# An 8-core encoder block on Trainium2: key latents multiplied from x times the norm's weight while x lands, with the root mean square applied afterwards

## The chip, the cores and the metric

The kernel runs on all 8 cores of one Trainium2 chip. Each core is given its own half of one sequence's queries (T = 1024 of S = 2048 tokens, batch 4) and works alone; no data goes between the cores. The metric is the time of one execution in microseconds (us) of the slowest core. The kernel before was run three times, 1668.05, 1668.99 and 1670.79 us; its median is 1668.99 us.

## The reference, cut to what matters

```
h = rmsnorm(x) * norm_g                       # over D = 2048 features
z = h @ w_in                                  # q_a (512), kv_a (256), k_pe (64), gates, conv inputs
q = rmsnorm(q_a, q_lat_g) @ w_uq              # 16 heads, own 1024 tokens
k, v = rmsnorm(kv_a, kv_lat_g) @ w_ukv        # 16 heads, all 2048 tokens
k_rope = k_pe, rotated by cos/sin(position)   # the "sine tables"
attn = softmax(q k) v ; conv branch ; gates ; two output projections
```

The change touches only the first two lines, for the columns kv_a and k_pe (the "key latents", 384 columns here with the rotated pair copied) and the sine tables. Since the norm is x * r(token) * norm_g(feature) with one r for each token, (x * norm_g) @ W * r is the same as h @ W, up to rounding.

## The kernel before, in words

All tensors lie transposed: features on the 128 partitions, tokens along the free dimension. x is read in four blocks of 512 tokens. Block 0 and 1 are the core's own tokens (queries and keys), 2 and 3 the other half (keys only). One block in float32 is 128 partitions x 16 feature chunks x 512 tokens (4 MB). There are two buffers, `xb[0]` for blocks 0 and 2 and `xb[1]` for blocks 1 and 3, so block 2 can be loaded once block 0 has been used up.

The program is a recording layer: each `P.op(engine, ...)` appends an instruction to its engine's queue in the order of the Python calls, and semaphore waits are derived from what is read and written. Every engine (PE, ACT, DVE, POOL, SP) executes its own queue strictly in that order. So the order of the work is the order in which the calls are written.

The first part, up to about 154 us, is what the change touches. Its helpers (line numbers are those of the kernel before):

- `load_x(blk, n)` (L327): the x block on SP's DMA queue in n pieces. `ld("pool", ...)` (L256) loads the weights `WlK` (key latents, 4 pieces) and `WlQ` (query latents, 4 pieces) from POOL's queue, which also turns float32 into bf16.
- `table(tab, posrow)` (L352 to L361): ten DVE instructions on 128x1024 float32 that depend on each other, then one sine on ACT (L362). `TABa` serves blocks 0 and 1 and the queries, `TABb` blocks 2 and 3.
- `A_sq(blk, j)`, j = 0 to 7: ACT squares two chunks of x (L383), and PE adds them up over the partitions with two matmuls by ones into bank `bB` (L385).
- `A_rs(blk)`: the factor r = exp(-0.5 ln(mean + eps)), two ACT instructions (L389, L390).
- `A_b(blk)`: sixteen DVE instructions `SCALAR_TENSOR_TENSOR` h = x * norm_g * r in bf16 (L401), into `hT` for blocks 0 and 1 (also used later by the gates and the convolution) and into `hTt` for blocks 2 and 3.
- `lat(blk, W, n, banks)`: 16 x n matmuls of 512 columns (L416), n = 3 for the key latents and 4 for the query latents, each waiting for its chunk of h.
- `e1_sq(blk)`: squares of the three key banks on ACT (L431, L445) and the product with the sine table on DVE (L446). `e1_mm` and `e2_mm` call `norm_of`: 2 or 4 matmuls by ones (L435), Ln and Exp on ACT (L436, L437), and 2 or 4 DVE instructions that write the normed latents (L439). `e1_ss` is four tiny matmuls (L454) and a copy (L456); `e1_cmb` a float32 matmul (L460) and an ACT copy (L461).
- `halo(blk)` (L407): one column of h of a neighbouring block, for the convolution.

The order before is, per block: all eight `A_sq`, `A_rs`, `A_b`, and only then `lat`. Both tables come first of all on DVE. The calls are L477 and the lines behind it: block 0's key latents, block 1's squares and norm, block 1's key latents, the two query latents (with block 2's squares in between), then the key latents of blocks 2 and 3. Behind them POOL's queue waits for x block 3 and loads the first weights of the next part (`load_kv`, `load_q`, `load_dense`), whose buffers `ring` overlay the position rows and `kf`, the scratch of `table`.

The next part (attention with convolution and gates mixed in, from L612 and L694 on) begins with the keys of head 0 directly behind the last `lat`; it and all that follows are not changed.

## Time and profile before

| | |
|---|---|
| median of three runs | 1668.99 us |
| the profiled execution's own time | 1669.85 us |
| its span on the slowest core (core 1) | 1668.3 us |
| spans of all 8 cores | 1662.0 to 1668.3 us |
| PE / DVE / ACT / POOL busy | 94% / 46% / 44% / 6% of the span |
| granted PE clock, mean | 0.987 of full on core 1 |
| data moved by DMA | 119.01 MB |

The span runs from the first to the last instruction of the profiled core; the execution's own time is 1.6 us longer, which lies around it. PE is the engine with the most work, and over the whole span it is nearly always busy. The first fortieths of the span (41.7 us each) are the exception: there the page shows PE busy 3, 6 and 9 tenths.

A row of the timeline reads: start, length, engine, line, operation, output<-input, shape, how many are merged, and in brackets the idle time of the engine before it and what ended that. Rows of groups give the number, the total, the mean of one, and the idle time ahead. Matmuls of 512 columns overlap, so two in a row last 0.59 us and each further one adds less than its own 0.38 us.

### The profile page before, as it was taken

To read this page: it belongs to the slowest core of one execution; us is meant where nothing else is said; L and a number is where in the kernel's file an instruction comes from. 1 tells how busy PE (TensorE), PEld (TensorE's weight loads), DVE (VectorE), ACT (ScalarE), POOL (GpSimd) and SP (SyncE) were. 2 spreads that over 40 slices of the span, in tenths; PEclk is the share of its full clock that TensorE was granted. 3 is DMA by queue.
4 is the path that set the end of the run, shared out by engine and by line. 5 is a ranking of instruction groups with operands and counts; after the bars stand their busy time and mean duration, and the time that the engine had idled before them with its cause. 6 is when DMAs were issued, how large, how long until landed. Compare 5 with 4: busy or idle time off the path is not lost.

```text
span 1668.3 us, 22689 instructions; the slowest of 8 cores (1662.0 to 1668.3 us)
## 1 busy us (share of the span) xinstructions
PE 1568.8 (94%) x7660; PEld 732.3 (44%) x7660; DVE 774.1 (46%) x999; ACT 737.8 (44%) x1234; POOL 94.1 (6%) x181
## 2 busy tenths in 40 slices
PE   3698999999999998999999999999999999999998
PEld 0144444444444444445445444444444444444443
DVE  6326377676666666776776211111111111243554
ACT  3344368777677777787776211011110101243211
POOL 0000000000000000000000110000100010000000
PEclk9799999999999999999999999999999999999999
DMA  9750321022101111211111673334433534974511
GB/s 253 207 123 13 58 39 33 7 36 35 33 14 32 33 27 20 39 28 18 20 26 26 120 143 60 70 65 87 84 69 69 89 70 85 222 165 80 119 69 70
DMA packets 37888, 119.01 MB, mean 71 GB/s; under 512 B 3984, under 2 KB 4112, under 8 KB 36240
## 3 DMA queue, kind: packets, MB, share of 16 engines
q0 software_dynamic: 25488, 82.85, 29.0%
q1 hardware_dynamic: 12288, 34.72, 6.4%
q8 instruction: 65, 1.06, 0.3%
q14 instruction: 47, 0.39, 0.1%
HBM read 192.00 MB, written 8.39 MB: 120 GB/s over the span
## 4 chain that ended last, share of the span: by engine, by line
PE 84%; ACT 5%; DVE 4%; issue 3%; DMA 2%; SPq 0%; ACTq 0%; DVEq 0%; POOL 0%; POOLq 0%
PE ps_o L833 5%; PE ps_s L773 5%; PE ps_s L775 5%; PE ps_s L968 4%; PE ps_s L930 3%; PE ps_o L891 3%; PE ps_s L900 3%; PE ps_s L872 3%; PE ps_s L894 3%; PE ps_s L891 3%; PE ps_a L900 3%; PE ps_o L894 3%; PE ps_s L416 2%; PE ps_a L694 2%; PE ps_b L897 2%
## 5 line engine op out<-in xcount | busy, mean ns | idle before, releaser
L780 ACT ACTIVATE arena<-ps_s,arena 128x512 bf16<-128x512 f32 x512 | 323.6, 685 | 50.7 <-PE ps_s L775 45.4
L820 DVE TENSOR_TENSOR arena<-arena 128x1024 f32<-128x1024 f32 x224 | 273.2, 1220 | 22.9 <-ACT arena L780 16.6
L773 PE MATMUL ps_s<-arena 128*128 128x512 bf16 x512 | 194.5, 380 | 9.8 <-ACT arena L780 9.5
L775 PE MATMUL ps_s<-arena 128*128 128x512 bf16 x512 | 194.5, 380 | 0.0
L833 PE MATMUL ps_o<-arena 128*128 128x512 bf16 x512 | 152.7, 380 | 1.2 <-ACT arena L836 1.2
L773 PEld LDWEIGHTS ps_s<-arena 128*128 128x128 bf16 x512 | 50.1, 98 | 78.2 <-issue 21.1
L775 PEld LDWEIGHTS ps_s<-arena 128*128 128x128 bf16 x512 | 50.1, 98 | 57.9 <-issue 0.7
L833 PEld LDWEIGHTS ps_o<-arena 128*128 128x128 bf16 x512 | 49.5, 98 | 39.4 <-issue 2.2
L903 ACT ACTIVATE arena<-ps_o 128x512 f32<-128x512 f32 x16 | 9.6, 597 | 129.3 <-PE ps_o L891 129.3
L905 DVE SCALAR_TENSOR_TENSOR arena<-arena,ps_s 128x512 f32<-128x512 f32 x16 | 11.0, 688 | 115.7 <-PE ps_s L897 115.7
L903 ACT ACTIVATE arena<-ps_s 128x512 f32<-128x512 f32 x16 | 9.6, 597 | 124.4 <-PE ps_s L891 124.4
L905 DVE SCALAR_TENSOR_TENSOR arena<-arena,ps_b 128x512 f32<-128x512 f32 x16 | 11.0, 688 | 115.4 <-PE ps_b L897 115.4
L953 ACT ACTIVATE arena<-arena 128x512 f32<-128x512 f32 x32 | 20.1, 629 | 97.4 <-DVE arena L952 97.4
L968 PE MATMUL ps_s<-arena 128*128 128x512 bf16 x272 | 62.8, 384 | 0.0
L875 DVE TENSOR_TENSOR arena<-arena 128x512 bf16<-128x512 bf16 x32 | 13.6, 426 | 95.6 <-ACT arena L874 95.6
L891 PE MATMUL ps_o<-arena 128*128 128x512 bf16 x256 | 57.9, 379 | 0.0
L891 PE MATMUL ps_s<-arena 128*128 128x512 bf16 x256 | 57.9, 379 | 0.0
L894 PE MATMUL ps_s<-arena 128*128 128x512 bf16 x256 | 57.9, 379 | 0.0
L900 PE MATMUL ps_s<-arena 128*128 128x512 bf16 x256 | 57.9, 379 | 0.0
L900 PE MATMUL ps_a<-arena 128*128 128x512 bf16 x256 | 57.9, 379 | 0.0
L894 PE MATMUL ps_o<-arena 128*128 128x512 bf16 x256 | 57.9, 379 | 0.0
L934 ACT ACTIVATE arena<-arena 128x512 bf16<-128x512 f32 x32 | 23.1, 721 | 77.5 <-DVE arena L933 77.5
(274 smaller groups left out, 2546.1 us busy)
## 6 DMA issues: line engine op xcount, KB each, us to landing
arena<-w_dense POOLq DMA_DIRECT2D x48, 512.0 KB, 5.4
arena<-w_merge POOLq DMA_DIRECT2D x48, 512.0 KB, 5.8
arena<-x_fm SPq DMA_DIRECT2D x20, 1024.0 KB, 24.7
arena<-w_pg POOLq DMA_DIRECT2D x16, 576.0 KB, 5.9
arena<-w_out POOLq DMA_DIRECT2D x16, 512.0 KB, 7.4
out<-arena SPq DMA_DIRECT2D x32, 256.0 KB, 2.0
arena<-x_fm SPq DMA_DIRECT2D x8, 512.0 KB, 13.3
arena<-w_q POOLq DMA_DIRECT2D x16, 256.0 KB, 3.5
```

The costliest lines, as they stand in the source:

```text
L416: "pe", lambda h: h.matmul(bks[m].ap, lhsT=W.ap[:, kc, m * 128:(m + 1) * 128], rhs=src, start=(kc == 0), stop=(kc == 15)),
L773: P.op("pe", lambda h, bk=bk, qs=qs: h.matmul(bk.ap, lhsT=Kb.ap[:, kt * 128:(kt + 1) * 128], rhs=Qa.ap[:, qs], start=True, stop=False), re ...
L775: P.op("pe", lambda h, bk=bk, qs=qs: h.matmul(bk.ap, lhsT=KrT.ap[:, kt * 128:(kt + 1) * 128], rhs=Qb.ap[:, qs], start=False, stop=True), r ...
L780: P.op("act", lambda h, sb=sb, qb=qb: h.activation(out=pt.ap[:, qb * 512:(qb + 1) * 512], in_=sb.ap, func=AF.Exp, scale=so.ap[:, kt:kt + 1 ...
L820: P.op("dve", lambda h, pt=pt, ac=ac: h.tensor_tensor(out=ac.ap, in0=ac.ap, in1=pt.ap, op=ALU.add), reads=R(ac, *pt.rl), writes=R(ac))
L833: P.op("pe", lambda h, qb=qb, kt=kt, pt=pt, hh=hh: h.matmul(Ow.ap[:, qb * 512:(qb + 1) * 512], lhsT=V.ap[:, kt, (hh % 2) * 128:(hh % 2) * ...
L872: P.op("pe", lambda h, kc=kc, bk=bk, sl=sl, ts_=ts_: h.matmul(bk.ap, lhsT=sl.ap[:, kc, :], rhs=hT.ap[:, kc, ts_], start=(kc == 0), stop=(k ...
L891: P.op("pe", lambda h, kc=kc, b_ma=b_ma, s_ma=s_ma, ts_=ts_: h.matmul(b_ma.ap, lhsT=s_ma.ap[:, kc, :], rhs=hT.ap[:, kc, ts_], start=(kc == ...
L894: P.op("pe", lambda h, kc=kc, b_mc=b_mc, s_mc=s_mc, ts_=ts_: h.matmul(b_mc.ap, lhsT=s_mc.ap[:, kc, :], rhs=hT.ap[:, kc, ts_], start=(kc == ...
L900: P.op("pe", lambda h, kc=kc, b_ya=b_ya, s_ba=s_ba, ts_=ts_: h.matmul(b_ya.ap, lhsT=s_ba.ap[:, kc, :], rhs=AT.ap[:, kc, ts_], start=(kc == ...
L930: P.op("pe", lambda h, kc=kc, bk=bk, sl=sl, ts_=ts_: h.matmul(bk.ap, lhsT=sl.ap[:, kc, :], rhs=merged.ap[:, kc, ts_], start=(kc == 0), sto ...
L968: P.op("pe", lambda h, kc=kc, bg=bg, sl=sl, ts_=ts_: h.matmul(bg.ap, lhsT=sl.ap[:, kc, :], rhs=h2T.ap[:, kc, ts_], start=(kc == 0), stop=( ...
```

## The change

1. **Order of loads.** POOL loads WlK at once (before: after the fifth piece of block 0). SP loads block 0's pieces 0 and 1, then the first position row, then pieces 2 to 7; block 1 comes in 8 pieces instead of 4; WlQ waits for the fifth of these eight; the second position row comes last.
2. **Key latents without the norm.** A new `A_x(blk, kc)` writes x * norm_g in bf16 (a `TENSOR_SCALAR` on DVE, L409 of the new file) into `hTt`, for all four blocks, and `lat(..., WlK, ...)` reads that. The matmuls no longer wait for r. In exchange `e1_sq` begins with three DVE instructions that multiply the three banks by r in place (L463). `A_b` (now L417, one chunk per call) remains for blocks 0 and 1 alone, and `halo` (L423, L424) works from x.
3. **Order of the work.** For every pair of chunks the calls are now: square, two `A_x`, then the six matmuls of these chunks, then the two sums of squares. Table A's ten instructions stand between the chunks of block 0. Block 0's latent norm and its sixteen `A_b` stand between the chunks of block 1, and behind them; block 1's `A_b` stand inside block 0's query latents. Table B moves behind `A_x` of block 2, its sine into block 3's squares. The loads of the next part's weights are written later, behind table B.

```diff
@@ -314,10 +314,10 @@
         Tpe = mk(196736, F32, [512], "Tpe")
         TABb = mk(198784, F32, [1024], "TABb")
         rq = mk(202880, F32, [512], "rq")
+        hgt = mk(204928, F32, [16, 1], "hgt")
 
         s_c = P.slot("consts")
         ld("sp", cols.ap, cols_d, cols, P.slot("cols"))
-        ld("sp", posrow[0].ap, pos_d[:, 0:1024], posrow[0], P.slot("pos0"))
 
         def load_x(blk, n=4, qs=None):
             b = xb[blk % 2]
@@ -331,17 +331,17 @@
             return last
 
         half = []
-        load_x(0, 8, range(3))
-        ld("sp", posrow[1].ap, pos_d[:, 1024:2048], posrow[1], P.slot("pos1"))
-        load_x(0, 8, range(3, 8))
-        half1 = half[0:1]
         for q in range(4):
-            ld("pool", WlK.ap[:, 4 * q:4 * q + 4, :], w_latk_d[:, 4 * q:4 * q + 4, :], WlK.rl[q], P.slot(f"wk{q}"), deps=half1)
+            ld("pool", WlK.ap[:, 4 * q:4 * q + 4, :], w_latk_d[:, 4 * q:4 * q + 4, :], WlK.rl[q], P.slot(f"wk{q}"))
+        load_x(0, 8, range(2))
+        ld("sp", posrow[0].ap, pos_d[:, 0:1024], posrow[0], P.slot("pos0"))
+        load_x(0, 8, range(2, 8))
         half[:] = []
         ld("sp", cmb.ap, cmb_d, cmb, s_c)
-        load_x(1)
+        load_x(1, 8)
         for q in range(4):
             ld("pool", WlQ.ap[:, 4 * q:4 * q + 4, :], w_latq_d[:, 4 * q:4 * q + 4, :], WlQ.rl[q], P.slot(f"wl{q}"), deps=half[0:1])
+        ld("sp", posrow[1].ap, pos_d[:, 1024:2048], posrow[1], P.slot("pos1"))
 
         P.op("dve", lambda h: h.memset(ones.ap, 1.0), writes=R(ones))
         P.op("dve", lambda h: h.memset(onesf.ap, 1.0), writes=R(onesf))
@@ -349,17 +349,19 @@
 
         def table(tab, pr):
             a, k = tab.ap, kf.ap
-            P.op("dve", lambda h: h.tensor_copy(out=a, in_=pr.ap), reads=R(pr), writes=R(tab))
...
-            P.op("dve", lambda h: h.tensor_scalar(out=a, in0=a, scalar1=PI_LO, scalar2=-PI_LO, op0=ALU.min, op1=ALU.max), reads=R(tab), writes=R(tab))
-            return lambda: P.op("act", lambda h: h.activation(out=a, in_=a, func=AF.Sin), reads=R(tab), writes=R(tab))
+            yield P.op("dve", lambda h: h.tensor_copy(out=a, in_=pr.ap), reads=R(pr), writes=R(tab))
...
+            yield P.op("dve", lambda h: h.tensor_scalar(out=a, in0=a, scalar1=PI_LO, scalar2=-PI_LO, op0=ALU.min, op1=ALU.max), reads=R(tab), writes=R(tab))
+
+        def sine(tab):
+            P.op("act", lambda h: h.activation(out=tab.ap, in_=tab.ap, func=AF.Sin), reads=R(tab), writes=R(tab))
 
         ring = [mk(82048 + 4096 * i, BF16, [16, 128], f"ring{i}") for i in range(4)]
         wq = [mk(208384, BF16, [4, 256], "wq0"), None]
@@ -381,36 +383,52 @@
         def A_sq(blk, j):
             b, sq = xb[blk % 2], sqx[j % 2]
             P.op("act", lambda h: h.activation(out=sq.ap, in_=b.ap[:, 2 * j:2 * j + 2, :], func=AF.Square), reads=R(b.rl[j]), writes=R(sq))
+
+        def A_ss(blk, j):
+            sq = sqx[j % 2]
             for i in range(2):
                 P.op("pe", lambda h, i=i: h.matmul(bB.ap, lhsT=ones.ap, rhs=sq.ap[:, i, :], start=(j == 0 and i == 0), stop=(j == 7 and i == 1)), reads=R(ones, sq), writes=R(bB))
+
+        def A_sqs(blk, j):
+            A_sq(blk, j)
+            A_ss(blk, j)
 
         def A_rs(blk):
             rs = rsb[blk % 2]
             P.op("act", lambda h: h.activation(out=rs.ap, in_=bB.ap, func=AF.Ln, bias=col(COL_EPS), scale=1.0 / D), reads=R(bB, cols), writes=R(rs))
             P.op("act", lambda h: h.activation(out=rs.ap, in_=rs.ap, func=AF.Exp, scale=-0.5), reads=R(rs), writes=R(rs))
 
+
+        def xsrc(blk, kc):
+            t = hTt[blk // 3]
+            return t.ap[:, kc, :], t.rl[kc]
+
+        def A_x(blk, kc):
+            b = xb[blk % 2]
+            dst, dres = xsrc(blk, kc)
+            P.op("dve", lambda h: h.tensor_scalar(out=dst, in0=b.ap[:, kc, :], scalar1=col(COL_NG + kc), scalar2=None, op0=ALU.mult), reads=R(b.rl[kc // 2], cols), writes=R(dres))
+
         def hsrc(blk, kc):
-            if blk < 2:
-                return hT.ap[:, kc, blk * 512:(blk + 1) * 512], hres(kc, blk)
-            return hTt[blk - 2].ap[:, kc, :], hTt[blk - 2].rl[kc]
-
-        def A_b(blk):
+            return hT.ap[:, kc, blk * 512:(blk + 1) * 512], hres(kc, blk)
+
+        def A_b(blk, c):
             b, rs = xb[blk % 2], rsb[blk % 2]
-            for c in range(16):
-                dst, dres = hsrc(blk, c)
-                P.op("dve", lambda h, c=c, dst=dst: h.scalar_tensor_tensor(out=dst, in0=b.ap[:, c, :], scalar=col(COL_NG + c), in1=rs.ap, op0=ALU.mult, op1=ALU.mult),
-                     reads=R(b.rl[c // 2], rs, cols), writes=R(dres))
+            dst, dres = hsrc(blk, c)
+            P.op("dve", lambda h: h.scalar_tensor_tensor(out=dst, in0=b.ap[:, c, :], scalar=col(COL_NG + c), in1=rs.ap, op0=ALU.mult, op1=ALU.mult),
+                 reads=R(b.rl[c // 2], rs, cols), writes=R(dres))
 
         def halo(blk):
-            t = hTt[blk - 2]
-            src, dst, m_ = (t.ap[:, :, 0:1], hT.ap[:, :, 1024:1025], COL_MR) if blk == 2 else (t.ap[:, :, 511:512], hT.ap[:, :, 1025:1026], COL_ML)
-            P.op("dve", lambda h: h.tensor_scalar(out=dst, in0=src, scalar1=col(m_), scalar2=None, op0=ALU.mult), reads=R(*t.rl, cols), writes=[hres(c, 2) for c in range(16)])
+            b, rs = xb[blk % 2], rsb[blk % 2]
+            t, c_, m_ = (0, 1024, COL_MR) if blk == 2 else (511, 1025, COL_ML)
+            P.op("dve", lambda h: h.tensor_tensor(out=hgt.ap, in0=b.ap[:, :, t:t + 1], in1=cols.ap[:, COL_NG:COL_NG + 16].rearrange("p (a b) -> p a b", b=1), op=ALU.mult), reads=R(*b.rl, cols), writes=R(hgt))
+            P.op("dve", lambda h: h.tensor_scalar(out=hT.ap[:, :, c_:c_ + 1], in0=hgt.ap, scalar1=rs.ap[:, t:t + 1], scalar2=col(m_), op0=ALU.mult, op1=ALU.mult),
+                 reads=R(hgt, rs, cols), writes=[hres(c, 2) for c in range(16)])
 
 
         def lat(blk, W, n, bks):
             out_ = []
             for kc in range(16):
-                src, sres = hsrc(blk, kc)
+                src, sres = xsrc(blk, kc) if W is WlK else hsrc(blk, kc)
                 for m in range(n):
                     out_.append(lambda kc=kc, m=m, src=src, sres=sres: P.op(
                         "pe", lambda h: h.matmul(bks[m].ap, lhsT=W.ap[:, kc, m * 128:(m + 1) * 128], rhs=src, start=(kc == 0), stop=(kc == 15)),
@@ -440,6 +458,9 @@
                      reads=R(bks[m], rq, cols), writes=R(dres))
 
         def e1_sq(blk):
+            rs = rsb[blk % 2]
+            for bk in (kbanks[blk][0], kbanks[blk][1], kbanks[blk][2]):
+                P.op("dve", lambda h, bk=bk: h.tensor_tensor(out=bk.ap, in0=bk.ap, in1=rs.ap, op=ALU.mult), reads=R(bk, rs), writes=R(bk))
             sq_of(kbanks[blk], 2)
             bp, tb_ = kbanks[blk][2], (TABa if blk < 2 else TABb)
             P.op("act", lambda h: h.activation(out=sqE.ap[:, 3, :], in_=bp.ap, func=AF.Square), reads=R(bp), writes=R(sqE.rl[3]))
@@ -472,29 +493,85 @@
         def e1_ins(blk):
             return [(9, lambda: e1_mm(blk)), (26, lambda: e1_ss(blk)), (32, lambda: e1_cmb(blk))]
 
-        table(TABa, posrow[0])()
-        sin_b = table(TABb, posrow[1])
+        def go(mms, lo, hi):
+            for f in mms[lo:hi]:
+                f()
+
+
+        tab = table(TABa, posrow[0])
         P.op("act", lambda h: h.activation(out=rq.ap[:, 0:1], in_=col(COL_EPS), func=AF.Ln), reads=R(cols), writes=R(rq))
+        mm = lat(0, WlK, 3, kbanks[0])
         for j in range(8):
             A_sq(0, j)
+            A_x(0, 2 * j)
+            A_x(0, 2 * j + 1)
+            if j > 1:
+                next(tab)
+            if j > 4:
+                next(tab)
+            go(mm, 6 * j, 6 * j + 6)
+            A_ss(0, j)
+        for _ in tab:
+            pass
         A_rs(0)
-        A_b(0)
+        sine(TABa)
+        e1_sq(0)
+
+
+        mm = lat(1, WlK, 3, kbanks[1])
+        for j in range(8):
+            A_sq(1, j)
+            A_x(1, 2 * j)
+            A_x(1, 2 * j + 1)
+            if j == 2:
+                e1_mm(0, banks[3])
+            elif j == 4:
+                e1_ss(0, banks[3])
+            elif j == 5:
+                e1_cmb(0)
+            if j != 2:
+                A_b(0, j if j < 2 else j - 1)
+            go(mm, 6 * j, 6 * j + 6)
+            A_ss(1, j)
+        A_rs(1)
+        for c in range(7, 11):
+            A_b(0, c)
+        e1_sq(1)
+        for c in range(11, 16):
+            A_b(0, c)
         load_x(2)
-        sin_b()
-        run(lat(0, WlK, 3, kbanks[0]), {})
-        e1_sq(0)
-        for j in range(3):
-            A_sq(1, j)
-        e1_mm(0, banks[3])
-        for j in range(3, 6):
-            A_sq(1, j)
-        e1_ss(0, banks[3])
-        e1_cmb(0)
-        for j in range(6, 8):
-            A_sq(1, j)
-        A_rs(1)
-        A_b(1)
+
+
+        mm = lat(0, WlQ, 4, qbanks[0])
+        go(mm, 0, 12)
+        e1_mm(1)
+        go(mm, 12, 20)
+        e1_ss(1)
+        go(mm, 20, 28)
+        e1_cmb(1)
+        for c in range(16):
+            A_b(1, c)
         load_x(3)
+        go(mm, 28, 64)
+        sq_of(qbanks[0], 4)
+        m4 = lat(1, WlQ, 4, qbanks[1])
+        mm = [m4[4 * kc + m] for kc in range(16) for m in range(3)] + m4[3::4]
+        go(mm, 0, 6)
+        e2_mm(0)
+        go(mm, 6, 16)
+        for j in range(8):
+            A_sqs(2, j)
+            A_x(2, 2 * j)
+            A_x(2, 2 * j + 1)
+            go(mm, 16 + 6 * j, 16 + 6 * j + 6)
+        A_rs(2)
+        sq_of(qbanks[1], 4)
+        tab = table(TABb, posrow[1])
+        for _ in tab:
+            pass
+        halo(2)
+        hTt.append(mk(32896, BF16, [16, 512], "hTt1"))
+        split(hTt[1], 16, "hTt1_")
         for i, b in enumerate(ring):
             b.slot = P.slot(f"ring{i}")
         wq[0].slot, wkv[0].slot = P.slot("wq0"), P.slot("wkv0")
@@ -504,22 +581,20 @@
         load_q(0)
         for s_ in range(4):
             load_dense(s_)
-        run(lat(1, WlK, 3, kbanks[1]), {})
-        e1_sq(1)
-        run(lat(0, WlQ, 4, qbanks[0]), ins(*e1_ins(1)))
-        sq_of(qbanks[0], 4)
-        m4 = lat(1, WlQ, 4, qbanks[1])
-        run([m4[4 * kc + m] for kc in range(16) for m in range(3)] + m4[3::4], ins((6, lambda: e2_mm(0)), *[(16 + 5 * j, lambda j=j: A_sq(2, j)) for j in range(8)]))
-        A_rs(2)
-        A_b(2)
-        sq_of(qbanks[1], 4)
-        halo(2)
-        hTt.append(mk(32896, BF16, [16, 512], "hTt1"))
-        split(hTt[1], 16, "hTt1_")
-        run(lat(2, WlK, 3, kbanks[2]), ins((5, lambda: e2_mm(1)), *[(14 + 4 * j, lambda j=j: A_sq(3, j)) for j in range(8)]))
+        mm = lat(2, WlK, 3, kbanks[2])
+        go(mm, 0, 5)
+        e2_mm(1)
+        go(mm, 5, 14)
+        for j in range(8):
+            A_sqs(3, j)
+            A_x(3, 2 * j)
+            A_x(3, 2 * j + 1)
+            if j == 1:
+                sine(TABb)
+            go(mm, 14 + 4 * j, 14 + 4 * j + 4)
+        go(mm, 46, 48)
         e1_sq(2)
         A_rs(3)
-        A_b(3)
         halo(3)
         run(lat(3, WlK, 3, kbanks[3]), ins(*e1_ins(2)))
         e1_sq(3)
```

At the start of PE's queue, before (L385 sums of squares, L416 key latents of block 0):

```order
L385 MATMUL ps_b<-arena 128x512 x16
L416 MATMUL ps_o<-arena 128x512 x2
L416 MATMUL ps_a<-arena 128x512
L416 MATMUL ps_o<-arena 128x512 x2
L416 MATMUL ps_a<-arena 128x512
```

The same place now (L434 is the latents' matmul, L390 the sum of squares):

```order
L434 MATMUL ps_o<-arena 128x512 x2
L434 MATMUL ps_a<-arena 128x512
L434 MATMUL ps_o<-arena 128x512 x2
L434 MATMUL ps_a<-arena 128x512
L390 MATMUL ps_b<-arena 128x512 x2
```

All sixteen sums stood ahead of the first latent matmul; now six latent matmuls and two sums alternate, eight times per block.

DVE's queue from the end of table A to block 1's norm, before (table B's ten stand directly ahead of the first row):

```order
L401 SCALAR_TENSOR_TENSOR arena<-arena 128x512 x16
L446 SCALAR_TENSOR_TENSOR arena<-ps_a,arena 128x512
L439 SCALAR_TENSOR_TENSOR arena<-ps_o,arena 128x512 x2
L456 COPY arena<-ps_s 128x4
L401 SCALAR_TENSOR_TENSOR arena<-arena 128x512 x16
```

And now, from the end of table A (L361) into block 1's chunks:

```order
L361 TENSOR_SCALAR arena<-arena 128x1024
L463 TENSOR_TENSOR ps_o<-ps_o,arena 128x512 x2
L463 TENSOR_TENSOR ps_a<-ps_a,arena 128x512
L467 SCALAR_TENSOR_TENSOR arena<-ps_a,arena 128x512
L409 TENSOR_SCALAR arena<-arena 128x512 x2
L417 SCALAR_TENSOR_TENSOR arena<-arena 128x512
L409 TENSOR_SCALAR arena<-arena 128x512 x2
L417 SCALAR_TENSOR_TENSOR arena<-arena 128x512
L409 TENSOR_SCALAR arena<-arena 128x512 x2
L457 SCALAR_TENSOR_TENSOR arena<-ps_o,arena 128x512 x2
L409 TENSOR_SCALAR arena<-arena 128x512 x2
L417 SCALAR_TENSOR_TENSOR arena<-arena 128x512
```

Here L463 and L467 of block 0 stand ahead of block 1's first L409, and block 0's L457 (the write of its latents, L439 before) ahead of block 1's chunks 6 and 7.

## Rows read from the trace of the kernel before

**Rows 1.** Windows of the first part: us, then PE busy, weight loads, DVE, ACT, POOL.
```profile
0.00:22.20 22.20, 0.00 (x0) 0.03 (x1) 13.60 (x19) 4.91 (x6) 1.59 (x7) 1.00 0.86 238
22.20:30.30 8.10, 5.87 (x16) 1.02 (x16) 4.05 (x5) 6.71 (x7) 0.87 (x2) 1.00 1.02 289
30.30:54.00 23.70, 15.46 (x48) 5.26 (x48) 10.69 (x16) 4.98 (x7) 2.12 (x4) 0.78 1.03 262
54.00:74.40 20.40, 10.33 (x24) 2.15 (x24) 3.23 (x6) 12.43 (x15) 0.00 (x0) 0.64 0.75 177
74.40:154.30 79.90, 75.02 (x328) 32.54 (x329) 42.37 (x65) 32.56 (x45) 4.24 (x8) 0.94 0.38 89
```

**Rows 2.** Timeline of PE, selected rows up to the first of the next part.
```profile
22.20 1.96 PE L385 MATMUL ps_b<-arena 128*128 128x512 bf16 x4 [22.20 <-ACT arena L383]
...
29.66 0.59 PE L385 MATMUL ps_b<-arena 128*128 128x512 bf16 x2 [0.35 <-ACT arena L383]
33.24 1.01 PE L416 MATMUL ps_o<-arena 128*128 128x512 bf16 x2 [2.98 <-DMA arena<-w_latk]
...
62.96 1.96 PE L385 MATMUL ps_b<-arena 128*128 128x512 bf16 x4 [3.87 <-ACT arena L383]
...
118.84 2.97 PE L416 MATMUL ps_s<-arena 128*128 128x512 bf16 x13
...
140.89 3.38 PE L416 MATMUL ps_s<-arena 128*128 128x512 bf16 x9 [3.54 <-DVE arena L401]
...
154.33 0.59 PE L612 MATMUL ps_s<-arena 128*128 128x512 bf16 x2
```

**Rows 3.** Timeline of DVE: the tables' ends, h of block 0, four latent writes.
```profile
16.47 0.69 DVE L361 TENSOR_SCALAR arena<-arena 128x1024 f32<-128x1024 f32 x1
...
23.85 0.69 DVE L359 TENSOR_SCALAR arena<-arena 128x1024 f32<-128x1024 f32 x1
...
25.98 0.69 DVE L361 TENSOR_SCALAR arena<-arena 128x1024 f32<-128x1024 f32 x1
31.88 10.69 DVE L401 SCALAR_TENSOR_TENSOR arena<-arena 128x512 bf16<-128x512 f32 x16 [5.20 <-ACT arena L390]
...
131.65 3.31 DVE L439 SCALAR_TENSOR_TENSOR arena<-ps_s,arena 128x512 bf16<-128x512 f32 x4
```

**Rows 4.** Timeline of SP and POOL: the first x issues, WlK and WlQ.
```profile
5.95 3.31 SPq L327 DMA_DIRECT2D arena<-x_fm  x5
...
20.81 2.25 POOL L256 DMA_DIRECT2D arena<-w_latk  x4 [20.12 <-DMA arena<-x_fm]
43.23 2.12 POOL L256 DMA_DIRECT2D arena<-w_latq  x4 [20.16 <-DMA arena<-x_fm]
```

**Rows 5.** DMA issues, landing in us: last piece of block 0, WlK's first and last.
```profile
arena<-x_fm SPq DMA_DIRECT2D x1, 512.0 KB, 16.9
...
arena<-w_latk POOLq DMA_DIRECT2D x1, 384.0 KB, 12.2
...
arena<-w_latk POOLq DMA_DIRECT2D x1, 384.0 KB, 27.5
```

**Rows 6.** Timeline of ACT: block 0's last squares, Ln, Exp, table B's sine.
```profile
25.63 3.89 ACT L383 ACTIVATE arena<-arena 128x1024 bf16<-128x1024 f32 x4 [0.31 <-PE ps_b L385]
30.35 0.69 ACT L389 ACTIVATE arena<-ps_b,arena 128x512 f32<-128x512 f32 x1 [0.83 <-PE ps_b L385]
31.13 0.63 ACT L390 ACTIVATE arena<-arena 128x512 f32<-128x512 f32 x1
31.78 1.28 ACT L362 ACT_TABLE_LOAD   x1
33.07 1.06 ACT L362 ACTIVATE arena<-arena 128x1024 f32<-128x1024 f32 x1
```

**Rows 7.** Groups of instructions on DVE by line and shape, whole span.
```profile
L682 DVE TENSOR_SCALAR arena<-arena 128x512 f32<-128x512 f32 x16 | 6.8, 426 | 10.4 <-ACT arena L725 10.4
...
L734 DVE TENSOR_TENSOR arena<-ps_a,arena 128x512 f32<-128x512 f32 x6 | 4.1, 686 | 0.9 <-PE ps_a L731 0.9
```

16 lines of the change are left out of this document (8 added, 8 removed).

## The prediction, written before the changed kernel was run

> **What bounds the kernel now.** I read the windows of the first part, then the timeline of PE, then what released its waits on DVE, ACT and the DMA queues. The kernel as a whole is bound by PE, but the part before attention is not. PE does nothing until 22.2 us. In the next 132.1 us its 416 matmuls [rows 1] need far less time: at the full clock one of 512 columns follows the other every 0.216 us, since thirteen in a row last 2.97 us, the last of them 0.38 [rows 2], and 400 of them are of that width, so 86 us. The rest is waiting and a low clock. PE first waits for squares (ACT's first square starts after table A's sine), then for WlK (2.98 us ahead of 33.24), then for block 1's squares (3.87 us ahead of 62.96), and 3.54 us at 140.89 for h of block 3 [rows 2]. After such an idle time the granted clock is the lower of its two levels (1.2 against 2.4 GHz): it reads 0.78, 0.64 and 0.94 of full in the three windows from 30.3 us on [rows 1], a pair of matmuls lasts about 1.01 us instead of 0.59, and nine take 3.38 us [rows 2]. So a matmul at the low level costs 0.427 us, 0.211 more. All of this ends at 154.33 us, where the next part's first matmul starts [rows 2]. That part finds the same work in the same order after the change, so **the question is only where 154.33 moves to**.
>
> **The change part by part.** I follow the queues with one price for each operation. Matmul 0.216 us; square 0.94 in a row (four in 3.89) and 1.06 alone; Ln 0.69, Exp 0.63, together 1.4 with the gap; table load 1.28 and sine 1.06 [rows 6]; `A_b` 0.66 (sixteen in 10.69); one table's ten instructions 9.5 (from 16.47 to 25.98), its last three 2.8 (from 23.85 to the end of 25.98); a latent write 0.83 (four in 3.31) [rows 3]. The trace of before has no `A_x`. Its bounds are 0.35 us (the 128x512 `TENSOR_SCALAR` of L682 lasts 0.43, and in a row some 0.08 overlaps, as 0.745 becomes 0.66 for L401) and 0.66 (the price of L401). I take 0.35, since L682 is the same operation on the same shape; only its output type differs [rows 7]. The product of a bank with r, in place, has 0.69 from L734 [rows 7]; twice that is my upper bound, since no row here writes a bank from DVE and reads it too. In the tables below each matmul count includes only what the calls list.
>
> *Loads.* Up to the last piece of block 0 (issued near 8.6 us, landed 16.9 later, so at 25.5 [rows 4, 5]) 5.3 MB had to come: 4.2 of x, 1.05 of positions. Now it is 6.3 MB: one position row less (0.52), all of WlK more (1.57). At 262 to 289 GB/s [rows 1] 1.0 MB costs 3.5 us. Before, WlK already took a part from 21 us on, so I take 3.0: **block 0 has landed at 28.5 us**. WlK's four pieces landed from 12.2 after 20.8 to 27.5 after 22.5, so every 5.7 us [rows 4, 5]; issued at 1 us they end near 25. So all of block 0's matmuls but the last few fit in between, as pieces come every 2.8 us and one piece's eight matmuls need 1.7 at full and 3.4 at low clock. Block 1 (4.2 MB) ends near 44.5 and is never waited for below.
>
> *A, block 0.* Last piece 28.5, square 1.06, two sums: PE has finished at 30.1. r is there at 31.6. DVE: two `A_x` 0.8, table A's last three 2.9, so 32.2; three products by r, 34.3. ACT: the sine with its table load runs 31.6 to 34.0, then three squares of about 0.55, 35.7. L467 stands next on DVE and waits for them, 0.8; and **block 1's first `A_x` is queued behind it** and ends at 37.0. PE resumes there after 6.9 us of idle, with at least four pieces of block 1 landed.
>
> *B, block 1.* 48 + 16 matmuls, the two by ones, the float32 one (0.9) and four tiny ones: 15.3 us. Block 0's Ln (with a table load back) and Exp end 2.8 us after the matmuls by ones; L457 follows (1.7), and block 1's chunks 6 and 7 are behind it on DVE: PE waits 3.3. Each of the two idle times costs twelve matmuls at the low level, as at 33.24 and 45 us before: 5.1. B is 23.7, to 60.7. In its second half DVE needs 1.4 us per pair of chunks, PE 1.7, so DVE is hidden; with an `A_x` of 0.66 it would need 2.0 and be the bound.
>
> *C, query latents of block 0.* 64 matmuls 13.8, ones and the float32 one 1.4, and 1.0 waiting for block 1's squares, which now follow two products by r: 16.2, to 76.9. The last five `A_b` of block 0 are done at 69, before their turn. WlQ, issued after the fifth piece (near 38) and sharing with x at one piece in 6 us, lands by 60, and x block 2 by 72.
>
> *D, query latents of block 1 with block 2's sums.* 64 + 16 + 4 matmuls 18.1, waits 1.3: 19.4, to 96.3. Block 1's `A_b` end near 81 and run ahead of PE. x block 3 waits for them and lands by 88.
>
> *E, key latents of block 2.* 48 + 16 + 4 matmuls 14.7, 1.4 for squares and r, 1.6 for table B's sine between block 3's squares (2.3 on ACT, partly hidden): 17.7, to 114.0. Table B's 9.5 us stand on DVE near 91 to 100; the latent writes of block 1 and sixteen `A_x` behind them end near 110. What hides them is E itself; if it were 4 us shorter they would show.
>
> *F, key latents of block 3.* 48 + 2 matmuls, float32 and tiny ones: 11.8. The matmuls by ones write `bB`, which Ln of block 3 must have read; that Ln stands behind three products, three squares and a table load: 2.6 us of waiting. To 128.4. At 140.89 before, nine matmuls went at low clock after such a wait [rows 2]; that would be 1.9 more, which I leave to the range.
>
> *Behind it.* Three products by r stand ahead of the last squares on DVE: 1.4 us later for what reads them. So 129.8 instead of 154.3: **24.5 us gained**. The weights of the next part are issued near 101 and need some 15 us, so they are there. The profiled execution took 1669.85, which gives 1645.4; it was 0.9 above the median of 1668.99, so **1644.6 us** is my number.
>
> **A rule against it.** The trace shows the low clock behind idle times, and a pair 0.35 us after the one before it at full clock (0.59 us at 29.66) [rows 2]. The Trainium skill, in "TensorE: Matmul & The Clock Gate", section "What's actually happening", says that the slow level is the default and that only activity releases it. By that rule a stream of short bursts, as A and B now are, can stay at the slow level. The trace agrees as far as it goes (0.64 in the window of bursts, 54 to 74.4 us). It is the first rival.
>
> **Rivals.**
> 1. *Bursts at low clock.* In A and B all matmuls go at 0.427 us. For: window 54 to 74.4 [rows 1]. Against: eight matmuls then take 3.4 us, more than the 2.8 between pieces, so PE is never idle there and nine to twelve such matmuls brought the clock back before [rows 2]. Price: 8 more in A, 40 more in B, 48 x 0.211 = 10, some of it instead of the 3.3 wait: 1652 us. Chance 0.17.
> 2. *DVE becomes the bound.* `A_x` costs 0.66, or a product by r 1.4. DVE then has 20 or 8 us more, of which about 7 shows (A 0.6, B 2.5, F 4, where block 3's `A_x` end too late). 1651 us. Chance 0.11.
> 3. *Less waiting than summed.* The pieces land at 27, one low stretch in B is missing and the wait there is half: 6 to 8 us. 1638 us. Chance 0.12.
> 4. *Slower than before: the clock stays low right up to attention.* 334 matmuls of 512 columns lie behind 37.0 us, 24 are already counted low; the gain is used up once 24.5 / 0.211 = 116 more go at the low level, and all 310 would cost 65 us, about 1710. Against: from 74.4 to 154.3 us the clock was 0.94 in spite of waits of 3.5 us [rows 1, 2]. Chance 0.04.
> 5. *No gain, because it returns as a wait.* The next part starts earlier but stands for its weights, whose issue moved behind table B: it decides once they land after 150 us, 49 after their issue, against 27.5 for the slowest piece of WlK [rows 5]. About 1669. Chance 0.03.
>
> **How the numbers follow.** The forecast has 0.53. The range reaches from rival 3 with its own spread to rivals 1 and 2 with one more low stretch: 1635 to 1656; outside it lie rivals 4 and 5 and the two tails. A measurement of this kernel can tell 0.2%, 3.3 us. Faster by more than that: forecast and rivals 1 to 3, 0.93. Within: 0.03. Slower: 0.04.
>
> **What would show it.** In the profile after: PE's first matmul well before 22 us; a hole of 6 to 8 us near 30, ended by L409; a second of about 3 us near 45, behind L457; 48 L434 of block 3 ending near 128, with a wait at L453 for ACT; L409 at 0.43 and L463 near 0.69 us; L689 (the next part's first) near 128. It would be wrong if the first part ended after 140, if a hole appears that DMA ends behind 40 us, or if the part behind it became longer by more than 3 us.

## The result, and the profile after

The changed kernel takes 1653.51 us (median of four runs, 1650.52 to 1655.10); the kernel before took 1668.99 us on the same chip (1668.05 to 1670.79). Some executions of every kernel are several per cent longer, with a lower granted clock on one or both dies (1709.18 us for the kernel before), and all medians here leave them out. The medians are 15.5 us apart. The estimated ratio is 0.9895, with a 95% interval of 0.9883 to 0.9908: about 1% faster. Forecast were 1644.6 us, with 1635 to 1656 as the range: right in its sign and inside the range, with a gain of somewhat under two thirds of what was summed (24.4 us).

The span of the slowest core went from 1668.3 to 1652.3 us, the mean of the eight cores from 1665.1 to 1649.1. The slowest core is now core 3. First, windows of its first part (us, then busy PE, weight loads, DVE, ACT, POOL, granted clock, DMA share, GB/s), which answer to [rows 1]:

```profile
0.00:12.80 12.80, 0.00 (x0) 0.00 (x0) 1.33 (x5) 2.54 (x3) 2.45 (x8) 1.00 0.79 153
12.80:43.80 31.00, 18.86 (x64) 7.03 (x65) 17.31 (x30) 14.04 (x16) 2.12 (x4) 0.85 1.02 292
43.80:82.00 38.20, 34.10 (x142) 14.38 (x143) 27.76 (x50) 14.60 (x19) 0.00 (x0) 0.90 0.71 176
82.00:134.00 52.00, 46.50 (x213) 20.18 (x212) 37.59 (x70) 32.53 (x41) 8.11 (x8) 1.00 0.62 137
```

PE's timeline, every row with over 0.8 us of idle time ahead and the first row of the next part, which answers to [rows 2]:

```profile
12.88 1.01 PE L434 MATMUL ps_o<-arena 128*128 128x512 bf16 x2 [12.88 <-DMA arena<-w_latk]
...
23.09 1.01 PE L434 MATMUL ps_o<-arena 128*128 128x512 bf16 x2 [4.32 <-DVE arena L409]
...
35.06 0.59 PE L434 MATMUL ps_o<-arena 128*128 128x512 bf16 x2 [0.89 <-DVE arena L409]
...
43.82 2.72 PE L434 MATMUL ps_s<-arena 128*128 128x512 bf16 x6 [6.87 <-DVE arena L409]
...
55.06 2.72 PE L434 MATMUL ps_s<-arena 128*128 128x512 bf16 x6 [3.31 <-DVE arena L409]
...
111.23 0.59 PE L390 MATMUL ps_b<-arena 128*128 128x512 bf16 x2 [1.51 <-ACT arena L385]
...
123.99 0.59 PE L453 MATMUL ps_b<-arena 128*128 128x512 bf16 x2 [2.46 <-ACT arena L398]
...
133.80 0.59 PE L687 MATMUL ps_s<-arena 128*128 128x512 bf16 x2
...
139.37 1.03 PE L777 MATMUL ps_b<-arena 128*128 128x342 bf16 x6 [2.23 <-ACT arena L454]
```

The next part starts at 133.80 us. On the mean of the eight cores it starts at 133.9 instead of 152.4 us, 18.5 earlier, and lasts 1515.3 instead of 1512.8 us, 2.5 longer. So 16.0 us remain. (These two means come from the first L612 or L687 on each core's timeline. Single edits below are compared by them: the intervals of their ratios mostly overlap that of the changed kernel, so their times alone don't tell them apart. Block 0 itself lands at 30.9 to 32.2 us in these profiles, so steps of under 1 us are not read.)

Three of the holes, the stretches in which PE stands idle, had been forecast by length and releaser: 6.9 us behind L409 (measured 6.87), 3.3 behind L409 (3.31) and 2.6 at L453 for ACT (2.46). The first two begin 6.8 us later than forecast. DVE's timeline shows what stands in front of that L409:

```profile
31.65 0.88 DVE L409 TENSOR_SCALAR arena<-arena 128x512 bf16<-128x512 f32 x2
32.44 1.22 DVE L357 SCALAR_TENSOR_TENSOR arena<-arena 128x1024 f32<-128x1024 f32 x1
33.76 0.75 DVE L358 TENSOR_SCALAR arena<-arena 128x1024 f32<-128x1024 f32 x1
34.43 0.88 DVE L409 TENSOR_SCALAR arena<-arena 128x512 bf16<-128x512 f32 x2
...
38.56 1.30 DVE L463 TENSOR_TENSOR ps_o<-ps_o,arena 128x512 f32<-128x512 f32 x2 [0.52 <-ACT arena L399]
39.76 0.69 DVE L463 TENSOR_TENSOR ps_a<-ps_a,arena 128x512 f32<-128x512 f32 x1
42.40 0.75 DVE L467 SCALAR_TENSOR_TENSOR arena<-ps_a,arena 128x512 f32<-128x512 f32 x1 [1.95 <-ACT arena L466]
43.07 1.00 DVE L409 TENSOR_SCALAR arena<-arena 128x512 bf16<-128x512 f32 x2
...
52.92 1.60 DVE L457 SCALAR_TENSOR_TENSOR arena<-ps_o,arena 128x512 bf16<-128x512 f32 x2 [5.95 <-ACT arena L455]
54.44 0.87 DVE L409 TENSOR_SCALAR arena<-arena 128x512 bf16<-128x512 f32 x2
...
90.17 6.42 DVE L409 TENSOR_SCALAR arena<-arena 128x512 bf16<-128x512 f32 x16
```

The first product by r (L463) waits 0.52 us for r, which ACT finishes 0.4 us after DVE has finished table A (L361, until 38.04). L467 waits 1.95 us for ACT, which had the sine and three squares to do; block 1's L409 stands behind it although its x had landed. Later, L457 waits 5.95 us for Ln and Exp, with L409 behind it again. Sixteen L409 in a row take 6.42 us, so 0.40 each (taken: 0.35, between 0.35 and 0.66), and L463 takes 0.69 by itself, as L734 in [rows 7].

Stage by stage on core 3, against the sum:

| | forecast | measured |
|---|---|---|
| block 0 landed | 28.5 | 31.8 (mean of cores 30.9) |
| PE ends block 0 | 30.1 | 36.9 (mean of cores 36.2) |
| block 1 begins (idle time) | 37.0 (6.9) | 43.8 (6.9) |
| B, key latents of block 1 | 23.7 | 22.5 |
| C, query latents of block 0 | 16.2 | 16.3 |
| D, query latents of block 1 | 19.4 | 18.9 |
| E, key latents of block 2 | 17.7 | 17.9 |
| F, key latents of block 3 | 14.4 | 14.4 |
| next part begins | 128.4 | 133.8 |

Core 3 doesn't show one thing. At L453 in F all eight cores wait 2.46 us, but on cores 0, 1, 5 and 7 the matmuls behind it go at the low clock for a while: seventeen take 4.95 to 5.52 us there and 3.83 on the other four. That costs these cores 1.5 to 1.7 us.

### The profile page after: what moved, and what is told of

Read it like the earlier page. It is cut to its first block, busy times and chain, and to the rows that moved or that the text cites. A ratio compares the mean times of both kernels' runs of the same rounds, so it can differ in the third digit from the quotient of the medians.

```text
span 1652.3 us, 22743 instructions; the slowest of 8 cores (1646.7 to 1652.3 us)
## 1 busy us (share of the span) xinstructions
PE 1564.8 (95%) x7660; PEld 734.1 (44%) x7660; DVE 785.6 (48%) x1045; ACT 740.3 (45%) x1235; POOL 98.0 (6%) x181
## 3 DMA queue, kind: packets, MB, share of 16 engines
q0 software_dynamic: 25488, 82.85, 29.4%
q1 hardware_dynamic: 12864, 34.72, 6.5%
HBM read 192.00 MB, written 8.39 MB: 121 GB/s over the span
## 4 chain that ended last, share of the span: by engine, by line
PE 84%; ACT 5%; DVE 5%; issue 4%; DMA 1%; SPq 0%; ACTq 0%; DVEq 0%
PE ps_o L908 6%; PE ps_s L848 5%; PE ps_s L850 5%; PE ps_s L1043 4%; PE ps_s L1005 3%; PE ps_s L975 3%; PE ps_s L969 3%; PE ps_s L947 3%; PE ps_o L969 3%; PE ps_o L966 3%; PE ps_s L966 3%; PE ps_a L975 3%; PE ps_s L434 2%; PE ps_a L769 2%; DVE arena L895 2%
## 5 line engine op out<-in xcount | busy, mean ns | idle before, releaser
L895 DVE TENSOR_TENSOR arena<-arena 128x1024 f32<-128x1024 f32 x224 | 273.3, 1220 | 24.1 <-ACT arena L855 18.3
```

What stands on the lines that cost most here:

```text
L895: P.op("dve", lambda h, pt=pt, ac=ac: h.tensor_tensor(out=ac.ap, in0=ac.ap, in1=pt.ap, op=ALU.add), reads=R(ac, *pt.rl), writes=R(ac))
```

## The experiments

The theories were: **D**, the landing of x and WlK sets the start; **O**, the order on DVE and ACT makes the holes; **C**, what counts is the low clock behind idle times. Every run has the kernel before beside it, on the same chip.

**1. The order of loads, alone and undone.** In the kernel before, WlK's loads were issued at once:

```diff
         half = []
+        for q in range(4):
+            ld("pool", WlK.ap[:, 4 * q:4 * q + 4, :], w_latk_d[:, 4 * q:4 * q + 4, :], WlK.rl[q], P.slot(f"wk{q}"))
         load_x(0, 8, range(3))
...
-            ld("pool", WlK.ap[:, 4 * q:4 * q + 4, :], w_latk_d[:, 4 * q:4 * q + 4, :], WlK.rl[q], P.slot(f"wk{q}"), deps=half1)
```

> The kernel before, with WlK's four loads issued at once instead of after the fifth piece of block 0; all else as before. Theory D (the loads set the start, and a load that turns float32 into bf16 costs the time of the 3.1 MB it reads, not of the 1.6 MB it writes): block 0 lands at 34 instead of 25.5 us, all of block 0's h comes 8 us later, the 7.3 us of waits for WlK go, block 1's squares are no longer waited for less: within 2 us of before, 1668 to 1671. Rival (bytes written count): block 0 lands at 29.5, the waits for WlK go, 4 to 5 us gained, 1664 to 1666. If the order of the loads alone were the gain of the change, it would be 1653.

Measured: 1669.51 us, ratio 0.9999 (0.9988 to 1.0009). Block 0 landed at 34.6 us on the mean of the cores instead of 24.6. That is the 34 of theory D, not the 29.5 of the rival. The gain of the change isn't in its loads.

And the changed kernel, with WlK, block 0 and the position rows loaded as before:

```diff
-        for q in range(4):
-            ld("pool", WlK...)
-        load_x(0, 8, range(2))
         ld("sp", posrow[0].ap, pos_d[:, 0:1024], posrow[0], P.slot("pos0"))
-        load_x(0, 8, range(2, 8))
+        load_x(0, 8, range(3))
+        ld("sp", posrow[1].ap, pos_d[:, 1024:2048], posrow[1], P.slot("pos1"))
+        load_x(0, 8, range(3, 8))
+        half1 = half[0:1]
+        for q in range(4):
+            ld("pool", WlK..., deps=half1)
...
-        ld("sp", posrow[1].ap, pos_d[:, 1024:2048], posrow[1], P.slot("pos1"))
```

> The changed kernel, with the order of WlK, block 0 and both position rows of before (WlK behind the fifth piece). Theory D: x lands at 25.5 but WlK's last piece near 50 us, and since sums of squares now stand behind the latent matmuls in PE's queue, PE ends block 0 near 52 instead of 36.9; some of that hides block 1's holes. First part 10 to 14 us longer than in the changed kernel, 1663 to 1668. Rival (the gain comes from the order of PE's and DVE's work and the loads don't matter): 1652 to 1656.

Measured: 1665.14 us, ratio 0.9966 (0.9953 to 0.9980). Block 0 lands at 24.1 us, but PE starts at 31.19 us with WlK's first piece, ends block 0 near 48, and the next part begins at 146.0, 12.1 later than in the changed kernel. So neither half of the change does it alone: all of the change but the order of loads is worth 0.34%, early WlK without the rest nothing.

**2. The two holes of block 1.** First, two pieces of block 1 ahead of the sine and the products of block 0, whose latent norm then comes one or two pieces later:

```diff
         A_rs(0)
+        mm = lat(1, WlK, 3, kbanks[1])
+        for j in range(2):
+            A_sq(1, j)
+            A_x(1, 2 * j)
+            A_x(1, 2 * j + 1)
+            go(mm, 6 * j, 6 * j + 6)
+            A_ss(1, j)
         sine(TABa)
         e1_sq(0)
...
-        for j in range(8):
+        for j in range(2, 8):
```

> The changed kernel, with block 1's first two pieces (squares, x times weight, matmuls) ahead of table A's sine and of block 0's products by r. Theory O (order on DVE and ACT sets the holes): PE resumes near 38.6 instead of 43.8, works 3.5 us, then waits near 4 us for the ninth L409 behind L467; net 1.3 to 2 us earlier at the end of block 1, 1651 to 1652.5. Rival C (the clock after a long idle time is what costs): the idle time ahead of the matmuls gets shorter than 2 us, the low stretch of 12 matmuls goes too and 4 us are gained. Rival D: nothing, 1653.5.

Measured: 1651.46 us, ratio 0.9887 (0.9871 to 0.9904); the next part begins at 131.0 instead of 133.9. PE's idle rows of core 3:

```profile
37.91 1.46 PE L434 MATMUL ps_s<-arena 128*128 128x512 bf16 x6 [1.64 <-DVE arena L409]
44.92 2.48 PE L434 MATMUL ps_s<-arena 128*128 128x512 bf16 x6 [3.39 <-DVE arena L409]
55.69 2.72 PE L434 MATMUL ps_s<-arena 128*128 128x512 bf16 x6 [2.59 <-DVE arena L409]
```

The hole of 6.87 us became one of 1.64, behind which six matmuls take 1.46 us (full clock), and one of 3.39, behind which they take 2.48 (low clock for most). The hole of 3.31 became 2.59, with six in 2.72 (low clock) behind it, and a small wait of 0.48. PE's waits in block 1 so fell from 10.2 to 8.1 us, and the two stretches of low clock are still there, 0.6 us shorter together. So 2.9 us were gained where theory O had 1.3 to 2, most of it idle time; the 4 us of rival C, with one stretch of low clock gone, did not come.

Then the writes of block 0's latents, taken out of `norm_of` and put behind block 1's chunks 6 to 9:

```diff
             if j == 2:
-                e1_mm(0, banks[3])
+                e1_mm(0, banks[3], late=True)
             elif j == 4:
+                e1_w(0)
                 e1_ss(0, banks[3])
```

> The changed kernel, with block 0's two latent writes (L457) behind block 1's chunks 6 to 9 on DVE instead of ahead of them. Theory O: the hole of 3.3 us at 55.1 goes, and with it the low-clock stretch behind it (2.6 us): first part 5 to 6 us shorter, 1647 to 1649. Rival (another wait takes its place: ACT's squares of block 1 stand behind Ln and Exp, so the sums wait instead): 1 to 2 us, 1651.5 to 1652.5.

Measured: 1649.91 us, ratio 0.9876 (0.9861 to 0.9891); the next part begins at 129.6, 4.2 us earlier. The hole of 3.31 us is gone, and the 1.7 us of low clock behind it; in its place PE waits 0.86 us for a square. Between the forecast of 5 to 6 and the rival of 1 to 2, nearer to the first.

**3. The end of block 0.** One instruction of table A per piece instead of two for the last three:

```diff
             if j > 1:
                 next(tab)
-            if j > 4:
-                next(tab)
```

> The changed kernel with one instruction of table A behind each pair of x times weight instead of two for the last three pieces; the others follow the last piece. Theory O: PE ends block 0 near 34 instead of 36.9, since the last pair on DVE no longer stands behind L357 and L358; r comes 2.5 us earlier, but table A ends at the same time, so block 1 starts only 1.5 to 2 us earlier: 1651.5 to 1652.3. Rival D (block 0's end is set by landing and the wait has another cause): 1653.5.

Measured: 1652.26 us, ratio 0.9891 (0.9875 to 0.9907). The time is at the edge of the forecast, but also within the noise of the changed kernel, and from block 0's landing to the next part it is 103.3 us instead of 102.9: no gain. The profile shows why (core 0, DVE and then PE):

```profile
40.37 0.69 DVE L361 TENSOR_SCALAR arena<-arena 128x1024 f32<-128x1024 f32 x1
40.98 1.29 DVE L463 TENSOR_TENSOR ps_o<-ps_o,arena 128x512 f32<-128x512 f32 x2
...
46.37 2.72 PE L434 MATMUL ps_s<-arena 128*128 128x512 bf16 x6 [7.71 <-DVE arena L409]
```

On the mean of the cores PE now ends block 0 3.9 us after its landing instead of 5.3, so the second instruction of table A per piece did hold PE back, by 1.4 us. But what was taken out there follows behind the last piece: L463 now starts directly behind L361, where it had waited for r in the changed kernel, and the hole ahead of block 1 grew from 6.8 to 8.0 us. Block 1's start thus hangs on two chains that are almost equally long, PE with r and DVE with table A, and shortening one alone gains nothing. The next run works on PE's chain and brings the third piece earlier:

```diff
-        for q in range(4):
+        for q in range(2):
             ld("pool", WlK...)
         load_x(0, 8, range(2))
+        half1 = P.ops["sp"][-1:]
+        for q in range(2, 4):
+            ld("pool", WlK..., deps=half1)
```

> The changed kernel, with WlK's pieces 2 and 3 issued only when block 0's second piece has landed. Theory A (block 0 ends late because PE stands from 18.8 to 23.1 us for the third piece and then needs 13.8 us for six pieces, two stretches of it at low clock; table A's instructions cost at most 0.9): the third piece lands 3 to 5 us earlier, PE ends block 0 near 34 instead of 36.9, 1650.5 to 1652. Rival 1 (table A on DVE sets the end of block 0): 1653.5. Rival 2 (WlK's last pieces then land 12 us after their issue, as in the kernel before, near 26 to 32, and PE waits for them): 1653 to 1656.

Measured: 1652.50 us, ratio 0.9907 (0.9891 to 0.9924), no gain; the next part begins at 133.9 as in the changed kernel. PE's rows of core 0:

```profile
19.35 0.59 PE L437 MATMUL ps_o<-arena 128*128 128x512 bf16 x2 [2.25 <-DVE arena L412]
...
26.70 1.01 PE L437 MATMUL ps_o<-arena 128*128 128x512 bf16 x2 [3.73 <-DVE arena L412]
...
35.41 0.59 PE L437 MATMUL ps_o<-arena 128*128 128x512 bf16 x2 [0.60 <-DVE arena L412]
...
44.04 2.72 PE L437 MATMUL ps_s<-arena 128*128 128x512 bf16 x6 [6.74 <-DVE arena L412]
```

The third piece came 3.3 us earlier on the mean of the cores (18.4 instead of 21.7 us), as intended, but then PE waited for the fifth, block 0's last piece landed 1.0 us later, and PE ended block 0 at 37.0 (36.2 in the changed kernel), so not near 34. The bytes ahead of the last piece are the same, and so is the last part of the way: on core 0 the last four pieces land within 6.6 us, PE comes out of an idle time of 3.73 us at low clock, and needs 3.4 us for the first of them, 2.9 for the second and 1.73 for the others.

**4. Behind the first part.** Block 3's products by r left out (its latents and rope key have no norm factor):

```diff
-            for bk in (kbanks[blk][0], kbanks[blk][1], kbanks[blk][2]):
+            for bk in ((kbanks[blk][0], kbanks[blk][1], kbanks[blk][2]) if blk < 3 else ()):
```

> The changed kernel without the three products by r of block 3 (L463); the latents and the rope key of block 3 are left without their norm factor. Theory G (these three products are why the part behind the last latent matmul is 2.5 us longer than before on the mean of the cores: they delay Ln of block 3, PE waits 2.2 us instead of 1.2 and some twenty matmuls behind it go at low clock): wait back to 1.2 us, no low stretch, the rest 1512.8 instead of 1515.3, 2.5 to 3 us gained, 1650.5 to 1651. Rival (the rest is longer for another reason, such as when weights land): 0.5 to 1 us.

Measured: 1649.00 us, ratio 0.9874 (0.9858 to 0.9889). The next part begins at 134.2, as in the changed kernel, but lasts 1511.5 us, 3.7 less. The rows that tell it, of core 7:

```profile
140.72 1.03 PE L777 MATMUL ps_b<-arena 128*128 128x342 bf16 x6 [1.20 <-ACT arena L454]
141.58 0.59 PE L687 MATMUL ps_s<-arena 128*128 128x512 bf16 x2
142.01 1.61 PE L777 MATMUL ps_b<-arena 128*128 128x342 bf16 x10
```

In the changed kernel (core 3) the same three are

```profile
139.37 1.03 PE L777 MATMUL ps_b<-arena 128*128 128x342 bf16 x6 [2.23 <-ACT arena L454]
140.24 0.90 PE L687 MATMUL ps_s<-arena 128*128 128x512 bf16 x2
140.92 3.04 PE L777 MATMUL ps_b<-arena 128*128 128x342 bf16 x10
```

One us more of waiting (2.23 instead of 1.20) is followed by the low clock, on all eight cores of the changed kernel and on none here, and the matmuls behind it cost another 1.7: ten of 342 columns in 3.04 instead of 1.61 us. These 2.7 us are what the products cost: on the mean of the cores the way from the next part's start to the next wait of over 2 us (L663, now L738) is 29.2 us before, 31.9 in the changed kernel and 29.2 here. The other 1.0 of the 3.7 us lies behind that point; the eight cores of the changed kernel differ there by 4.5 us among themselves, so it is not put down to the products.

Ln and Exp of block 3's r ahead of block 2's bank squares (the two calls swapped, `A_rs(3)` before `e1_sq(2)`):

> The changed kernel with r of block 3 (Ln, Exp) ahead of block 2's bank squares on ACT. Theory: the wait of 2.46 us at L453 in block 3's latent matmuls is for the read of the shared bank by Ln; it goes, but the squares come 1 us or so later: 1.5 to 2.5 us gained, 1651 to 1652. Rival (squares become the wait): 0 to 0.5 us.

Measured: 1648.63 us, ratio 0.9871 (0.9853 to 0.9889), more than the 1.5 to 2.5 us that were expected; the next part begins at 130.7, 3.2 us earlier, and lasts 1.7 us less. The 2.46 us at 123.99 became 0.18, so the wait was for Ln's read of the shared bank. With it went the low clock that had followed on four of the eight cores, 0.8 us on the mean. And at L777, where the wait is 2.22 us as in the changed kernel, only three of the eight cores now fall to the low clock, which gives 1.0 of the 1.7 us; why the others don't is not shown.

**5. All of it.** Block 1's pieces come right behind block 0's; the products, the rest of table A, the sine and the late writes stand between them; r of block 3 comes first, with its table load brought forward by a one-column Ln; and block 3's matmuls for banks 0 and 1 come ahead of those for bank 2, so that their products by r are hidden behind sixteen matmuls.

```diff
+            if j in (0, 2, 3, 4):
+                next(tab)
+            if j == 1:
+                e1_r(0)
+            elif j == 4:
+                sine(TABa)
...
+            elif j == 5:
+                e1_w(0)
+            elif j == 6:
+                e1_t(0)
...
-        run(lat(3, WlK, 3, kbanks[3]), ins(*e1_ins(2)))
+        m3 = lat(3, WlK, 3, kbanks[3])
+        run([m3[3 * kc + m] for kc in range(16) for m in range(2)] + m3[2::3], ins(*e1_ins(2)))
```

> The changed kernel with all of it: one table instruction per piece, block 1's chunks never queued behind a wait (products, sine, latent writes of block 0 spread between its pieces), r of block 3 first with its table load ahead, and block 3's matmuls ordered so that banks 0 and 1 end 16 matmuls early. If the holes are independent: 3 (table) + 6.9 and 3.3 (holes) + 2 x 2.6 (low stretches) + 2.5 (F) + 2.7 (G), less 3 for waits that come in their place: 17 us, 1636 to 1639. Rival (DVE is then the bound for h of block 0 and the query latents wait): 8 to 11 us, 1642 to 1645. If landing of x were the bound, 1650.

Measured: 1637.60 us, ratio 0.9804 (0.9789 to 0.9820). That is within the forecast of 1636 to 1639. The next part begins at 122.4 and lasts 1511.9 us. PE's idle times of over 2 us left on core 5:

```profile
23.82 1.01 PE L434 MATMUL ps_o<-arena 128*128 128x512 bf16 x2 [4.92 <-DVE arena L409]
...
51.05 0.59 PE L390 MATMUL ps_b<-arena 128*128 128x512 bf16 x2 [2.58 <-ACT arena L385]
...
103.26 1.01 PE L390 MATMUL ps_b<-arena 128*128 128x512 bf16 x2 [2.34 <-ACT arena L385]
```

The last two are the sines, which stand between squares on ACT. They are moved to places where ACT waits (`sine(TABa)` behind block 1's `A_rs`, `sine(TABb)` behind `e1_mm(2)`), with the first position row behind block 0's fourth piece, table A's instructions from the fifth piece on, and the matmuls for the last bank of block 0's query latents behind those for the other three:

> The kernel e8_best, with both sines moved to where ACT waits anyway (table A's into the query latents of block 0, table B's into the last key latents), the first position row behind block 0's fourth piece, and table A's instructions one per piece from the fifth piece on. If the two holes left at 46 to 51 us (2.6) and 98 to 103 us (2.3) are the sines' 2.3 us on ACT between squares, both go: 4 to 5 us gained on 1637.6, and up to 2 more where the third piece lands earlier: 1631 to 1634. Rival (DVE is now the bound and block 0's h comes too late for the query latents): 1636 to 1639.

Measured: 1636.13 us, ratio 0.9806 (0.9790 to 0.9823). The forecast of 1631 to 1634 is missed. Both holes are gone and the next part begins at 118.8, 3.6 us earlier; new waits of 1.8 us (for L409, in block 1) and 1.3 us (for squares behind the sine, in block 0's query latents) took their place. The two kernels were measured on different chips, and their ratios (0.9804 and 0.9806) don't part them; of the 3.1 us between the mean spans of their profiles (1634.4 and 1631.3) 1.3 may be the chip's, since the kernel before took 1670.2 beside the one and 1668.9 beside the other. Either is 1.8 to 2.1% faster than the kernel before, and both beat the changed one.

## Why the prediction was right, and where it was not

- **What bounds the kernel, and that only 154.33 moves**: right but for 2.5 us, below.
- **The range held partly by luck.** The measured time lies where rivals 1 and 2 stood (1652 and 1651), and the upper part of the range was there for them. What filled it, the landing and the backlog of block 0, was no rival's.
- **Loads: mis-sized.** The step was "At 262 to 289 GB/s 1.0 MB costs 3.5 us", with WlK counted at the 1.57 MB that it writes. Experiment 1 measured WlK's cost by itself: 10.0 us of block 0's landing, so 157 GB/s of written bytes, or 315 of the 3.15 MB of float32 that it reads. The page had shown it, in both kernels. Its third section, of the changed kernel (packets, MB, share of 16 engines), and the line below it:

```profile
q0 software_dynamic: 25488, 82.85, 29.4%
q1 hardware_dynamic: 12864, 34.72, 6.5%
...
HBM read 192.00 MB, written 8.39 MB: 121 GB/s over the span
```

  119 MB are moved but 192 MB read; a MB of the converting queue takes 0.294 x 1652.3 / 82.85 = 5.9 us, one of the other 3.1. (The converting queue's 82.85 MB twice, and the plain queue's 34.72 less the 8.39 written to HBM, are 192.0 MB.) Priced like that, WlK adds 9.3 us and the missing position row takes off 1.6, so block 0 would land 7.7 us later. The forecast had 3.0; measured were 6.3 on the mean of the cores (24.6 to 30.9). On core 3 the error is 3.3 us.
- **"All of block 0's matmuls but the last few fit in between": wrong, by as much again.** I had an even stream, a piece every 2.8 us. The third piece landed at 22.4 us (issued at 2.9, 19.5 us to landing), the eighth at 31.8 on core 3. PE idled for 4.32 us (4.2 to 6.8 on the eight cores), came back at low clock, and then had six pieces to do, 13.8 us: 10.4 at full clock, 2.3 more for the low one, 0.9 of waiting for L409 behind table A. So PE ended block 0 5.1 us after its landing, where the sum had 1.6. With the landing this made A's end 36.9 instead of 30.1, 6.8 us. Run e6 showed that table A on DVE has 1.4 us of this backlog, and that taking it away gains nothing while the rest of table A follows. Run e10 left the backlog at 5.1 us on the mean of the cores (5.3 in the changed kernel); that a smoother landing would end block 0 earlier was not shown.
- **A's idle time, B and its two low stretches, C, D, E, F**: right on core 3, each within 1.2 us, the mechanisms included. B is 1.2 us shorter since its stretch of low clock behind 3.31 us has eight matmuls, not twelve. The trace of before had shown that: the matmuls from 45.05 us on, named as an example of twelve, have eight low ones. F's low stretch of 1.9 us, left to the range, came on four of the eight cores. Runs e3, e4 and e7 took out or shortened three of the waits, and moved the next part's start by 2.9, 4.2 and 3.2 us, each within 1 us of what had been expected of it.
- **Behind it, 1.4 us: mis-sized.** It was 2.5 on the mean of the cores. PE waits 1.0 us longer there, where 1.4 had been summed; the low clock that follows, 1.7 us, was left out. Run e5 showed 2.7 us in all for these products.
- **The base.** I took the start of the next part on core 1 (154.33). The mean of the cores was 152.4, 1.9 earlier. Forecast gain 24.5, less 5.5 for the first part, less 1.1 behind it, less 1.9 for the base: 16.0, which is what the mean of the cores gained.
- **The signs** came as named: PE's first matmul at 12.88 us, the three waits, the first part over at 133.8 us, no hole behind 40 us that DMA ended, and a part behind it that is 2.5 us longer, with 3 as the limit. (L689, named as the next part's first line, is DVE's; PE's is L687.)
- **Rivals.** Bursts at low clock: no; the window 12.8 to 43.8 us stands at 0.85, and on core 3 up to 134 us only the first matmuls and those behind idle times of over 3 us are low (on four other cores also those behind 2.46 us). The rule that the prediction cites from the Trainium skill, "TensorE: Matmul & The Clock Gate", section "What's actually happening", that activity releases the slow level, agrees with these rows: the clock comes back within the first dozen matmuls of each burst. DVE as the bound: through its order (and, as e6 shows, through table A ahead of block 1), not through the price of `A_x` or of the products. Less waiting than summed, slower than before, waiting for the next part's weights: not seen.

## What to carry to other kernels

Work made independent of a late factor starts early only if nothing that waits for this factor stands ahead of it in any engine's queue: here block 0's L467 and L457, which wait for ACT, stood ahead of block 1's L409 on DVE, and PE stood idle for 10 us behind them. The order on DVE, ACT and PE together was worth about as much again as the change itself (15 to 16 us more in e8). Where two chains of nearly equal length meet, as PE's and DVE's at the end of block 0, shorten both or neither. Price a converting load by what it reads, and look at the third section of the page before a sum of bytes. A wait that lowers the clock costs twice, so a product or a copy ahead of the first matmuls of a new part should be hidden behind matmuls of another bank.
